# The RWKV recurrence as one step with two alternating groups, 32-row chunk products on parts of the array, and small loads issued one step earlier

## The reference

```python
def step(state, inp):
    r_t, w_t, k_t, v_t, a_t, b_t = inp
    sa = jnp.einsum('bhvk,bhk->bhv', state, a_t)
    state = (state * w_t[:, :, None, :] + sa[..., None] * b_t[:, :, None, :]
             + v_t[..., None] * k_t[:, :, None, :])
    return state, jnp.einsum('bhvk,bhk->bhv', state, r_t)
...
_, y = lax.scan(step, state0, xs)
```

## Time and profile before

| | |
|---|---|
| median of 3 runs | 3993.22 us (3987.27 to 3993.67) |
| the profiled execution | 3981.06 us |
| its span, first to last instruction | 3979.1 us |
| TensorE busy | 3140.8 us, 79% of the span |
| VectorE busy | 2424.2 us, 61% |
| ScalarE busy | 797.4 us, 20% |
| mean granted TensorE clock | 0.898 |

### The profile page before, as it was taken

One profiled execution on the slowest core, in us unless ns is written; L12 is line 12 of the kernel. 1 busy time (PEld: TensorE's weight loads), 2 busy tenths in 40 slices (PEclk: granted clock), 3 DMA queues, 4 the chain that ended last, 5 costly groups with the idle time before them and its releaser, 6 DMA issues. The chain is left out here.

```text
span 3979.1 us, 45873 instructions
## 1 busy us (share of the span) xinstructions
PE 3140.8 (79%) x17432; PEld 2433.3 (61%) x17432; DVE 2424.2 (61%) x4431; ACT 797.4 (20%) x1927; POOL 581.6 (15%) x516
## 2 busy tenths in 40 slices
PE   7674767878877877677887789976767899994798
PEld 7573763334334867533433359965746899983798
DVE  4352667667665536666666758654335777765586
ACT  1313222222222122222222220112201201012300
POOL 0000014444442000243443410000000000000000
PEclk8896889989998989898998899978977999996899
DMA  5141359999996524699999966523002565650364
GB/s 190 55 138 51 127 200 405 402 395 410 403 400 262 170 80 133 253 397 394 403 395 402 401 237 181 164 88 118 27 1 77 145 186 166 181 165 24 106 177 147
DMA packets 469258, 860.94 MB, mean 216 GB/s; under 512 B 18736, under 2 KB 398384, under 8 KB 402352
## 3 DMA queue, kind: packets, MB, share of 16 engines
q0 software_dynamic: 73728, 536.90, 33.2%
q1 hardware_dynamic: 395168, 319.59, 26.2%
q10 hardware_dynamic: 144, 1.52, 0.1%
HBM read 849.56 MB, written 8.39 MB: 216 GB/s over the span
## 5 line engine op out<-in xcount | busy, mean ns | idle before, releaser
L2018 PE MATMUL banks<-arena,arena 128*128 128x512 f32 x2048 | 1009.8, 653 | 317.7 <-ACT arena L2071 317.7
L2018 PEld LDWEIGHTS banks<-arena,arena 128*128 128x128 f32 x2048 | 419.7, 209 | 891.4 <-issue 505.0
L2170 DVE CUSTOM_DVE_ANT_0 arena<-arena,normed 128x1024 f32<-128x1024 f32 x512 | 620.5, 1222 | 412.5 <-DMA arena<-in_peer_uv,arena 412.4
L1980 POOL DMA_INDIRECT arena<-in_peer_uv,arena x512 | 581.4, 1135 | 1747.9 <-DVE arena L2153 966.9
L301 DVE TENSOR_TENSOR weight_ring_part<-weight_ring,weight_high_parts 128x2048 fp32r<-128x2048 f32 (+3 forms) x258 | 572.0, 2217 | 8.8
L2563 PE MATMUL banks<-normed_columns_part,weight_high_parts 128*128 128x256 f32 x1408 | 402.7, 286 | 11.3 <-PEq L249 9.5
L2564 PE MATMUL banks<-normed_part,weight_high_parts 128*128 128x256 f32 x1408 | 401.0, 285 | 0.0
L2565 PE MATMUL banks<-normed_columns_part,weight_ring_part 128*128 128x256 f32 x1408 | 400.8, 285 | 0.0
L298 DVE CAST weight_high_parts<-weight_ring 128x2048 fp32r<-128x2048 f32 (+3 forms) x258 | 305.4, 1184 | 153.7 <-PE banks L576 90.3
L574 PE MATMUL banks<-weight_high_parts,arena_part 128*128 128x256 f32 x1216 | 347.0, 285 | 43.2 <-PEq L249 31.2
L575 PE MATMUL banks<-weight_ring_part,arena_part 128*128 128x256 f32 x1216 | 344.5, 283 | 0.0
(11 more groups left out here) (469 smaller groups left out, 4305.0 us busy)
## 6 DMA issues: line engine op xcount, KB each, us to landing
weight_ring<-in_ffn_w_gate SPq DMA_DIRECT2D x88, 512.0 KB, 4.0
weight_ring<-in_ffn_w_up SPq DMA_DIRECT2D x88, 512.0 KB, 5.2
weight_ring<-in_ev_w_in SPq DMA_DIRECT2D x33, 1024.0 KB, 5.4
weight_ring<-in_ffn_w_down SPq DMA_DIRECT2D x32, 1024.0 KB, 5.2
weight_ring<-in_od_w_in SPq DMA_DIRECT2D x23, 1024.0 KB, 5.4
weight_ring<-in_xa_wkv SPq DMA_DIRECT2D x16, 1024.0 KB, 5.7
weight_ring<-in_peer_wq SPq DMA_DIRECT2D x16, 1024.0 KB, 5.7
weight_ring<-in_ev_w_out SPq DMA_DIRECT2D x12, 1024.0 KB, 5.4
```

The lines of the kernel that those rows point to most:

```text
L1980: pool.indirect_dma_start(out=ring[:, slot(i, s), :], out_offset=None, in_=table, in_offset=bass.IndirectOffsetOnAxis(ap=index[:, i % 2, s ...
L2018: mm = pe.matmul(k.ps[:, 2 * b + half, :], diag[:, n % 2, s, :], v, start=h == 0 and g == 0 and s == 0, stop=h == PEER_HEADS - 1 and g == ...
L2170: dve.tensor_tensor_reduce(out=ring[:, here, 0:D], in0=ring[:, here, 0:D], in1=k.xn[:, b, :], scale=1.0, scalar=0.0, op0=ALU.mult, op1=ALU ...
```

## The change

`recurrence`, from the transpositions on, becomes **one step**: all engines follow a fixed order with a semaphore for each kind of hand-over. The two blocks of 128 tokens are two groups of 8 units. In each level TensorE first multiplies for group 0, then squares for it, then does one bank of the output grams, then the same for group 1; so one group's results are copied while the other group is multiplied. The last squaring keeps only the matrix that is used, and two of its four banks carry the transposes of `end` and `ke`. The masked copies are gone: each move and input is a product of 32 rows (one chunk) and 64 columns (one head) on the part of the array at those rows. States and moves are kept per head (64 x 64). The read-out goes per head as well, and `read` and `add_own` produce columns at once, with no transposition.

```diff
+            def take_step(l, g):
+                ...
+                for i in range(2):
+                    for n in range(4):
+                        u = 8 * g + 4 * i + n
+                        mm = pe.matmul(step_bank(i)[:, n * P:(n + 1) * P], powers[:, u, 1, :], both(u), start=True, stop=True)
+                    mm.then_inc(k.rw_stepped.sem, 1)
...
+            def moves(b):
+                ns = chunks_of(b, 1, n_chunks - 2)
+                for h in range(8):
+                    for n in ns:
+                        c = n % per_block * C
+                        mm = pe.matmul(own_head(move_bank(n), h)[:, h // 2 * H:(h // 2 + 1) * H],
+                                       solved[c:c + C, b, 0, h * H:(h + 1) * H], rows[c:c + C, b, BE, h * H:(h + 1) * H],
+                                       start=True, stop=True)
+                        if h == 7:
+                            mm.then_inc(k.rw_moved.sem, 1)
...
+            def move_state(n):
+                ...
+                for h in range(8):
+                    mm = pe.matmul(own_head(state_bank(n), h)[:, h // 2 * H:(h // 2 + 1) * H], own_head(moveT, h)[:, n, h // 2, :],
+                                   own_head(states, h)[:, n - 1, h // 2, :], start=True, stop=True)
+                mm.then_inc(k.rw_scanned.sem, 1)
...
+            def give_out(ns):
+                for j in range(4):
+                    for h in (2 * j, 2 * j + 1):
+                        for n in ns:
+                            o = own_head(out_bank(j // 2), h)[:, j % 2 * T + n * C:j % 2 * T + (n + 1) * C]
+                            mm = pe.matmul(o, own_head(states, h)[:, n - 1, j, :], own_head(reader, h)[:, j, n * C:(n + 1) * C],
+                                           start=True, stop=True)
+                return mm
             for b in range(NB):
+                for i, columns in enumerate((kk, val)):
+                    ...
+                    rows_turned(columns, b, k.ps[:, i, :]).then_inc(k.rw_turned.sem, 1)
+                fed_grams(b)
+                step_grams(b)
+            for b in range(NB):
+                feed_values(b)
+            for l in range(levels):
+                for g in range(NB):
+                    take_step(l, g)
+                    if l < levels - 1:
+                        square(l, g)
+                        output_grams(2 * l + g)
+            ...
+            moves(0)
+            ...
+            inputs(0)
+            ...
+            moves(1)
+            ...
+            inputs(1)
+            move_state(1)
+            read(0)
+            move_state(2)
+            read(1)
+            move_state(3)
+            add_own(0)
+            move_state(4)
+            add_own(1)
+            move_state(5)
+            ...
+            give_out(range(1, n_chunks - 2))
+            move_state(n_chunks - 2)
+            ...
+            give_out(range(n_chunks - 2, n_chunks)).then_inc(k.rw_out.sem, 1)
```

The loads move into the `columns_out` or `rows_out` step before, ahead of the ring's own loads on SyncE's queue (`also`):

```diff
@@ even_mixer
+    k.columns_out(k.hT, [512] * 3, lambda e, m, bank: e.tensor_tensor(padded[:, m, 3:], bank, k.wide[:, :], ALU.mult),
+                  also=lambda sp: k.fetch_memory_rows(sp, "mem", memory_rows))
...
+    def fetch_heads(sp):
+        for i, name in enumerate(("ml_wq", "ml_wk", "ml_wv")):
+            sp.dma_start(wqkv[:, i], k.ins[name][0].rearrange("h (c p) e -> p (h c) e", p=P)).then_inc(k.heads_in.sem, 16)
+            k.heads_in.adds(16)
+        k.fetch_memory_rows(sp, "mem", memory_rows)
...
@@ rwkv
-    with k.step() as block:
-        @block.vector
-        def _(dve):
-            dve.memset(w2[:, 0:2, :], 0.0).then_inc(k.vector_done.sem, 1)
-            dve.wait_ge(k.vector_done.sem, k.vector_done.next())
-    with k.step(side=4) as block:
...
-    with k.step(side=1) as block:
+    with k.step(side=5) as block:
         @block.tensor
         def _(pe):
+
+            pe.wait_ge(k.heads_in.sem, k.heads_in.total)
             for m in range(12):
```

More of the change, by code:

```diff
@@ L1114, in even_mixer @@
     padded = k.take(12, T + 3)
+    memory_rows = k.take(NB, D)
     zero_front(k, padded, 3)
@@ new lines, in two, with four, both, own_head @@
+    def two(m):
+        u = m // 4 * 8 + m % 4 // 2 * 4 + m % 2
+        return u, u + 2
+    def four(m):
+        return [m // 2 * 8 + m % 2 + 2 * i for i in range(4)]
+    def both(u):
+        return solved[:, u // 8, :, u % 8 * H:(u % 8 + 1) * H]
+    def own_head(ap, h):
+        return ap[h % 2 * H:h % 2 * H + H]
+    def square_bank(n):
+        return k.ps[:, (2, 3, 4, 0, 1)[n % 5], :]
+    def step_bank(i):
+        return k.ps[:, 6 + i, :]
+    def move_bank(n):
+        return k.ps[:, (n - 1) % 3 + 1, 0:4 * H]
@@ L2949, in recurrence, with rows_turned, fed_grams @@
-    with k.step() as block:
+            def rows_turned(columns, b, bank):
+                for c in range(4):
+                    mm = pe.transpose(bank[:, c * P:(c + 1) * P], columns[:, c, b * P:(b + 1) * P], k.c("ident"))
+                return mm
+            def fed_grams(g):
+                for i in range(2):
+                    if g:
+                        pe.wait_ge(k.rw_masked.sem, k.rw_masked.start + i + 1)
+                    for n, u in enumerate(four(2 * g + i)):
+                        mm = pe.matmul(k.ps[:, 6 + i, n * P:(n + 1) * P], head(key, u), head(kk, u), start=True, stop=True)
+                    mm.then_inc(k.rw_grammed.sem, 1)
@@ L3035, in recurrence @@
-    reader, own = kk, rate
-    k.to_columns(mixed[:, :, 0, :], 4, reader)
-    k.to_columns(mixed[:, :, 1, :], 4, own)
-    with k.step() as block:
+                for i, dst in enumerate((solved[:, b, 0, :], rows[:, b, V, :])):
+                    act.wait_ge(k.rw_turned.sem, k.rw_turned.start + 2 * b + i + 1)
+                    act.activation(dst, k.ps[:, i, :], ACT.Copy).then_inc(k.rw_rows.sem, 1)
+            for b in range(NB):
+                act.wait_ge(k.rw_fed.sem, k.rw_fed.start + b + 1)
+                act.activation(solved[:, b, 1, :], k.ps[:, b, :], ACT.Copy).then_inc(k.rw_fed_kept.sem, 1)
@@ L3039, in _ @@
+            act.activation(y[:, :, 0:C], own[:, :, 0:C], ACT.Copy).then_inc(k.scalar_done.sem, 1)
+            k.scalar_done.next()
         @block.vector
         def _(dve):
[L3041 to L3048 removed]
@@ L3157, in recurrence, with mask_fed @@
-    with k.step() as block:
-        @block.vector
-        def _(dve):
-            dve.tensor_copy(y[:, :, 0:C], own[:, :, 0:C]).then_inc(k.vector_done.sem, 1)
-            dve.wait_ge(k.vector_done.sem, k.vector_done.next())
+            def mask_fed(g):
+                for i in range(2):
+                    dve.wait_ge(k.rw_grammed.sem, k.rw_grammed.start + 6 * g + i + 1)
+                    u = four(2 * g + i)[0]
+                    dve.tensor_tensor(mT[:, u:u + 7:2, :], k.ps[:, 6 + i, :].rearrange("p (u t) -> p u t", u=4),
+                                      mid(k.c("strict32T"), 4), ALU.mult).then_inc(k.rw_masked.sem, 1)
@@ new lines, in _ @@
+            for n in (1, 2, 3):
+                keep_move(n)
+            add_state(1)
+            keep_move(4)
+            add_state(2)
+            keep_move(5)
+            keep_reader(0)
+            add_state(3)
+            keep_move(6)
+            keep_reader(1)
+            add_state(4)
+            add_state(5)
+            add_state(6)
+            dve.wait_ge(k.rw_own.sem, k.rw_own.start + 2)
+            dve.wait_ge(k.rw_out.sem, k.rw_out.start + 1)
+            for i in range(2):
+                s_ = slice(2 * i, 2 * i + 2)
+                dve.tensor_tensor(y[:, s_, C:], out_bank(i).rearrange("p (j t) -> p j t", j=2)[:, :, C:], own[:, s_, C:],
+                                  ALU.add).then_inc(k.vector_done.sem, 1)
+                k.vector_done.adds(1)
```

612 lines of the change are left out of this document (306 added, 306 removed).

## The result

The changed kernel took 3840.1 us (median of four runs, 3839.1 to 3843.9); the kernel before, on the same chip, 3990.2 us (3983.3 to 3993.7). The ratio is 0.9628, 95% interval 0.9611 to 0.9644: 3.7% faster. The forecast was 3866 us with a range of 3846 to 3908, so the sign was right and the time is 5.9 us under the range. The mechanism forecast is there. What was mis-sized is the tail of the new step.

The account below looks back on a forecast made before the run. Bound by an order in which engines wait for each other, finally by TensorE at 1.2 GHz. Recurrence saves 86.0 us (111.5 against 197.5), with loads 127.6: 3981.1 becomes 3853.5, plus 12.1 gives 3866 us, range 3846 to 3908.

Parts of the forecast that it names:

- the tail: End of the new step, with moves, inputs, states and read-out: products and waits sum to 44.4 us.
- The early loads: Small loads issued earlier for memories, mLSTM heads, RWKV's low-rank part and the DSA part: 41.6 us saved.
- the heads' idle time: TensorE's wait before the mLSTM heads: 5.1 us instead of 16.59, so 11.5 us saved.
- The front: Start of the new step, with TensorE's transpositions, grams and value products: 13.2 us.
- The levels: Step products, squares, output grams and transpositions of the new step, with a bank wait and mode changes: 53.9 us.
- the output grams: In the levels, 32 products of 64 rows at 0.157 us each: 5.0 us.
- the 2.6 for changes: In the levels, TensorE changes 16 times between full and 64-row products, 0.16 us each: 2.6 us in all.
- the 264 small ones: Tail products of 32 or 64 rows and 64 weight columns, at 0.12 us without overlap: 31.7 us.
- the three things by which it was to be wrong: TensorE waiting for ScalarE in the levels, clock falling after the last level, small products 110 ns or more a record.
- The parts overlap fully: Rival for the tail: 160 products at 0.06 us and no drains, 12 us less, 3854 us; chance 0.12.
- Two row halves of one bank take turns: Rival for state moves and read-out: 104 products at 0.225 us instead of 0.12, 3877 us; chance 0.08.
- The tail runs at 1.2 GHz: Rival for the tail: the 39.9 us of products double at the lower clock, 3906 us; chance 0.18.

Follow-up runs that it names:

- one chunk after the other: Changed kernel with the loops of moves and inputs turned round, all heads of one 32-row chunk before the next; the step took 101.5 us.
- states' products early: Changed kernel with each state's product queued as soon as its operands can be there, VectorE's order adapted; 3835.4 us, ratio 0.9602.
- the gap before the tail: Changed kernel with two VectorE reciprocals of 128 x 1024 before its last additions of the levels, so TensorE stands still; the step took 112.5 us.

## Why the prediction was wrong

**Right.** The sign, and the reading of the old step: the order bounds it, and at its end the clock. The early loads: 43 us by stages against 41.6, with the heads' idle time at 5.08 against 5.1. The front: 13.3 us against 13.2. The levels: 56.2 against 53.9, with TensorE 98% busy, and the wait for the bank of group 1 there once, 0.9 us. The term there that was off is the output grams. They were priced at 0.157 from a row in which a bank of one half of the array is followed by a bank of the other; here a call is one bank, and both its heads lie on the same half. In order of time:

```profile
2799.94 0.49 PE L3047 MATMUL banks<-arena,arena 64*128 64x128 f32 x2
2800.26 0.38 PE L3048 MATMUL banks<-arena 64*128 64x128 f32 x2
2800.49 0.38 PE L3047 MATMUL banks<-arena,arena 64*128 64x128 f32 x2
2800.71 0.38 PE L3048 MATMUL banks<-arena 64*128 64x128 f32 x2
2801.02 0.71 PE L3007 MATMUL banks<-normed,arena 128*128 128x128 f32 x4
```

Four products take 1.08 us, changes of mode included, so eight calls cost 8.6 us where 5.0 and a part of the 2.6 for changes were set.

**The step that failed** is in the tail: "I take 0.12 for the 264 small ones, since both what is loaded and what is streamed is half of the 0.225 row, and count no overlap: 31.7". The price alone is right: in one chunk after the other, records of one place come 0.058 us apart, 0.12 a product. The overlap was left out, although the rows that the price came from (64 rows at 0.157) were themselves evidence of it. Measured in the first profile: 160 moves and inputs in 6.0 us less 1.8 of a stop, 0.026 each; a state's eight products with their halves 6 ns apart, 0.058 each; the read-out near 0.07. Together 160 x 0.026 + 48 x 0.058 + 56 x 0.07 = 10.9 us instead of 31.7. The 48 products of 128 rows took 0.11 each (5.3 us, forecast 8.2). So 16.2 us of products instead of 39.9, and 9.3 us of waits instead of 4.5; of the 4.8 more, 3.3 are the two stops for instructions, which no term foresaw. The forecast's own signs show the miss: records of 32 rows were to come about 60 ns apart and came 13 ns apart, and one of the three things by which it was to be wrong, a clock that falls after the last level, happened in two of three profiles.

**The rivals.** "The parts overlap fully" (0.12) is what happened, but its price stopped at 160 products and at 0.06 each, a quarter of the full product for a load of half the columns. A 32 x 64 product uses an eighth of the array, and six to eight such parts were used in turn here. "Two row halves of one bank take turns" (0.08) did not happen: the state products of both halves write one bank and start 6 ns apart. The rule of the Trainium skill (TensorEngine Tiling (Array Packing), Gotcha 1: PSUM Pressure) isn't refuted by it, since the halves also write different partitions, which that sentence does not speak of; the forecast had stretched it to a case it doesn't name. No run here lets two row halves write the same partitions of one bank. "The tail runs at 1.2 GHz" (0.18) came true for 10 us in most profiles, at 3.5 us. Its other ground, that these products could not raise the clock, doesn't hold: wherever the clock fell in the tail, it was back at 2.4 GHz 7 to 17 us later, inside the tail.

**The range.** Its lower end, 3846, took in the 12 us of the overlap rival, 8 for misfit and nothing for the basis. The sum was put on the median of before with the saving of one short execution, whose recurrence took 197.5 us where two other profiles have 199.5 and 203.3. Of the 26 us between forecast and median, the step is 13 (98.4 us against 111.5), the longer old step 2 to 6, the loads 1 to 2, and 3 are the median of before, 3993.2 in the forecast and 3990.2 with a fourth run. The remaining 2 to 7 us are within the spread of the measurements (150 and 157 us between medians); which stretch they come from stays open. Also open is what part the stops for instructions have in the fall of the clock. One chunk after the other shows a fall without any stop, so they aren't needed for it; no run here fed TensorE faster.

## What to carry to other kernels

When a kernel is recast into small products on parts of the array, price them twice: by the pace within one part, and by that pace over the number of parts that neighbours in the queue use in turn, and let the range hold both. The second is a lower bound: two halves in turn gave it (0.058 of 0.12), six to eight parts in turn would give 0.015 to 0.02 and 0.026 was measured. Then count instructions: here a packet brought those of 64 products and packets came 3.2 to 4.4 us apart, 0.05 to 0.07 us a product, so a long run of cheaper products stops for them. Whether an order that mixes small products with long ones gains by it is not shown: the one tried (states' products early) had a first stop of 0.3 us, and its time can't be told from the changed kernel's. And take the basis from more than one profile: the old step took 197.5, 199.5 and 203.3 us in three.

## What the hardware showed that was not expected

- TensorE ran out of instructions, as the counts of records have it: stops of 1.0 to 2.0 us with no semaphore behind them, after 201 to 204 and then 128 records, each ending 2.2 to 2.9 us after a 16 KB instruction packet starts. Packets came no closer than 3.2 us.
- Products of 32 x 64 weights over 64 columns, on row groups and column halves in turn, start at 0.026 us a product; with the same row group again and again, 0.048.
- In the gap before the tail, the granted clock came back to 2.4 GHz 0.5 us into the small products, behind eight full ones at half speed. It fell in the tail after 8.0 us in which TensorE was busy 4.9, and did not after the same 8.0 us with the same 4.9 in the first profile; with one chunk after the other it fell while TensorE was busy without a gap.
- One kernel's executions spread over 20 us, and two profiles of it differ by 5.8 us in a stretch whose code is the same, with 92 us of it at 1.2 GHz against 75.
